# Two-layer hybrid decoder on one core: a first group that starts without the low halves, an output projection by column blocks, and rotary embedding wholly on VectorE

## What is computed

```
h = rms_norm(x, attn_norm); proj = h @ w_in                  # 1024 x 3072
q, k of 16 heads of 64 get the rotary embedding:
    out = concat([x1*cos - x2*sin, x2*cos + x1*sin])
out_a = rms_norm(causal attention of heads 0-7); out_d = rms_norm(dilated attention of heads 8-15)
x = x + concat([out_a, out_d]) @ w_out                       # 1024 x 1024
x = x + square(relu(rms_norm(x, mlp_norm) @ w_up)) @ w_down  # 1024 x 4096 x 1024
```

## Time and profile before

| | |
|---|---|
| runs shown | 598.18, 599.14, 599.41 us, median 599.14 |
| the profiled execution | 599.35 us, span of the instructions 597.6 us |
| PE busy | 584.8 us, 98% of the span |
| DVE busy | 401.6 us, 67% |
| ACT busy | 313.9 us, 53% |
| POOL busy | 62.5 us, 10% |

### The profile page before, as it was taken

One profiled execution on the slowest core, in us unless ns is written; L12 is line 12 of the kernel. 1 busy time (PEld: TensorE's weight loads), 2 busy tenths in 40 slices (PEclk: granted clock), 3 DMA queues, 4 the chain that ended last, 5 costly groups with the idle time before them and its releaser, 6 DMA issues.

```text
span 597.6 us, 9254 instructions
## 1 busy us (share of the span) xinstructions
PE 584.8 (98%) x3326; PEld 491.1 (82%) x3326; DVE 401.6 (67%) x649; ACT 313.9 (53%) x532; POOL 62.5 (10%) x67
## 2 busy tenths in 40 slices
PE   8999999999999999999999999999999999999995
PEld 5879876788888888888888898778888888888884
DVE  3896986588655655755389968767775755755634
ACT  4846767465634534435186646774654435435322
POOL 0070240110000000000005225001100000000001
PEclk8999999999999999999999999999999999999999
DMA  8946343437756466465245634440877465465201
GB/s 306 362 143 212 99 160 95 141 129 252 253 182 238 142 200 220 145 237 180 71 161 192 212 100 183 141 141 13 268 247 247 143 220 199 151 231 179 106 0 70
DMA packets 58844, 104.20 MB, mean 174 GB/s; under 512 B 1808, under 2 KB 35136, under 8 KB 58816
## 3 DMA queue, kind: packets, MB, share of 16 engines
q1 hardware_dynamic: 58320, 103.03, 51.3%
q10 hardware_dynamic: 496, 0.81, 0.5%
HBM read 102.79 MB, written 1.05 MB: 174 GB/s over the span
## 4 chain that ended last, share of the span: by engine, by line
PE 88%; DVE 4%; ACT 4%; issue 2%; DMA 1%; POOL 1%; POOLq 0%; ACTq 0%; DVEq 0%
PE psum L1164 20%; PE psum L952 15%; PE psum L954 14%; PE psum L953 14%; PE psum L1167 10%; PE psum L973 6%; PE psum L978 3%; PE psum L1099 2%; PE psum L1119 1%; PE psum L1137 1%; PE psum L959 1%; ACT w_hi L498 1%; DVE w_lo L670 1%; DMA x<-in_x 1%; PE psum L1140 1%
## 5 line engine op out<-in xcount | busy, mean ns | idle before, releaser
L670 DVE TENSOR_TENSOR w_lo<-raw,w_hi 128x1024 fp32r<-128x1024 f32 x188 | 228.5, 1248 | 50.9 <-ACT w_hi L498 50.9
L498 ACT CAST w_hi<-raw 128x1024 fp32r<-128x1024 f32 x188 | 186.6, 1048 | 0.4 <-PE psum L978 0.3
L1164 PE MATMUL psum<-xt,w_hi 128*128 128x512 f32 x512 | 160.7, 395 | 0.0
L952 PE MATMUL psum<-w_hi,ot_hi 128*128 128x512 f32 x320 | 127.2, 397 | 1.5 <-ACT v L566 1.5
L953 PE MATMUL psum<-w_lo,ot_hi 128*128 128x512 f32 x320 | 124.8, 390 | 0.0
L954 PE MATMUL psum<-w_hi,ot_lo 128*128 128x512 f32 x320 | 124.7, 390 | 0.0
L1167 PEld LDWEIGHTS psum<-xt,w_lo 128*128 128x128 f32 x512 | 96.2, 188 | 22.4
L1167 PE MATMUL psum<-xt,w_lo 128*128 128x256 f32 x512 | 100.6, 278 | 0.0
L1164 PEld LDWEIGHTS psum<-xt,w_hi 128*128 128x128 f32 x512 | 80.2, 189 | 2.4
L614 ACT COPY up_cross<-psum 128x512 f32<-128x512 f32 x32 | 18.8, 587 | 118.7 <-PE psum L1167 118.7
L845 DVE TENSOR_TENSOR up_cross<-psum,up_cross 128x512 f32<-128x512 f32 x32 | 22.1, 691 | 74.1 <-ACT up_cross L614 74.1
(11 more groups left out here) (91 smaller groups left out, 593.8 us busy)
## 6 DMA issues: line engine op xcount, KB each, us to landing
raw<-in_w_up SPq DMA_DIRECT2D x32, 1024.0 KB, 5.6
raw<-in_w_down SPq DMA_DIRECT2D x32, 1024.0 KB, 6.7
raw<-in_w_in SPq DMA_DIRECT2D x21, 1024.0 KB, 5.2
raw<-in_w_out SPq DMA_DIRECT2D x8, 1024.0 KB, 4.8
raw<-in_w_in SPq DMA_DIRECT2D x3, 512.0 KB, 8.1
raw<-in_w_in SPq DMA_DIRECT2D x4, 256.0 KB, 4.8
out<-x SPq DMA_DIRECT2D x3, 256.0 KB, 2.4
x<-in_x SPq DMA_DIRECT2D x2, 256.0 KB, 4.8
```

Source lines behind the costliest of these rows:

```text
L498: act.copy(dst, src).then_inc(hi_done, 1)
L670: dve.tensor_tensor(lo_t, src, hi_t, ALU.subtract).then_inc(split_done, 1)
L952: pe.matmul(out, s_hi, m_hi, start=first, stop=False)
L1164: pe.matmul(up_banks[b][:, f, :], w_hi[:, slot, cols[f]], xt[:, k, :, :].rearrange("p a b -> p (a b)"), start=k == 0, stop=False)
```

## The change

It touches five places. (1) The first six tiles of group 0 in layer 0 are multiplied in the order high x, low weights, low x, with the 512-column matmul in two of 256; four zero matmuls ahead (zero weights) clear the banks; DVE makes each tile's low weights before the low x. (2) `ROPE_ROW` goes from step 10 to 11 and the rotary table entries from 11, 12, 13 to 12, 13, 14. (3) The rotary products become one operation of 1024 elements and their sum one of 512, both on DVE; the table that they read has four rows (cos, cos, sin, minus sin), written by three operations; POOL has no part in it. (4) The output projection of steps 48 to 55 goes t, n, k instead of t, k, n, and frees its four units in the last block. (5) The turning of the last four heads' probabilities and the last product with v come one step later, and squares are always taken one step after the high part.

```diff
-PT_AT = {s + 3: h for s, h in QK_AT.items()}
-PV_AT = {29: (0, 1), 42: (2, 3), 50: (4, 5), 55: (6, 7)}
+PT_AT = {s + 3 + h // 12: h for s, h in QK_AT.items()}
+PV_AT = {29: (0, 1), 42: (2, 3), 50: (4, 5), 56: (6, 7)}
-SQUARES_LATE = {56: (6, 7)}
+SQUARES_LATE = {30: (0, 1), 43: (2, 3), 51: (4, 5), 57: (6, 7)}
-SUM_AT = {8: (0, 0), 9: (0, 1), 12: (1, 0), 16: (1, 1), 36: (4, 0), 40: (4, 1)}
+SUM_AT = {8: (0, 0), 9: (0, 1), 14: (1, 0), 16: (1, 1), 36: (4, 0), 40: (4, 1)}
-ROPE_ROW = 10
-ROPE_AT = {11: (0, 0), 12: (0, 1), 13: (1, 0), 17: (1, 1), 28: (3, 0), 32: (3, 1), 37: (4, 0), 41: (4, 1)}
+ROPE_ROW = 11
+ROPE_AT = {12: (0, 0), 13: (0, 1), 14: (1, 0), 17: (1, 1), 28: (3, 0), 32: (3, 1), 37: (4, 0), 41: (4, 1)}
...
-            def rope_sum(l, g, hg):
-                j = ROPE_GROUPS[g]
-                pool.wait_ge(rope_terms, qk_half(l, g, hg) + 1)
...
-                pool.tensor_tensor(dst[:, 0, :], a[:, 0, :], b[:, 1, :], ALU.subtract)
-                pool.tensor_tensor(dst[:, 1, :], a[:, 1, :], b[:, 0, :], ALU.add).then_inc(rope_done, 1)
...
-                dve.tensor_tensor(rope_r[:, :, :], rope_tab[:, :, :],
-                                  row_bank[:, 0:SEQ].unsqueeze(1).broadcast_to([P, 2, SEQ]), ALU.mult)\
-                    .then_inc(rope_scaled, 1)
+                row = row_bank[:, 0:SEQ].unsqueeze(1)
+                dve.tensor_tensor(rope_r[:, 0:2, :], rope_tab[:, 0:1, :].broadcast_to([P, 2, SEQ]),
+                                  row.broadcast_to([P, 2, SEQ]), ALU.mult)
+                dve.tensor_tensor(rope_r[:, 2:3, :], rope_tab[:, 1:2, :], row, ALU.mult)
+                dve.scalar_tensor_tensor(out=rope_r[:, 3:4, :], in0=rope_tab[:, 1:2, :], scalar=-1.0, in1=row,
+                                         op0=ALU.mult, op1=ALU.mult).then_inc(rope_scaled, 1)
...
-                dve.tensor_tensor(a, raw_qk, cos, ALU.mult)
-                dve.tensor_tensor(b, raw_qk, sin, ALU.mult).then_inc(rope_terms, 1)
+                terms = rope_a[:, :, :].rearrange("p a (i t) -> p a i t", i=2)
+                dve.tensor_tensor(terms, raw_qk.broadcast_to([P, 2, 2, SEQ]),
+                                  rope_r[:, :, :].rearrange("p (a i) t -> p a i t", a=2), ALU.mult).then_inc(rope_terms, 1)
+                if l > 0 or j > 1:
...
+                dve.wait_ge(rope_terms, n + 1)
+                dve.tensor_tensor((q_t, k_t)[j % 2][:, hg, :, :], terms[:, 0, :, :], terms[:, 1, ::-1, :], ALU.add)\
+                    .then_inc(rope_done, 1)
...
                     for k in range(4):
+                        tile_to_lo(k)
                         x_lo(k)
-                        tile_to_lo(k)
...
                 pe.wait_ge((tile_hi, hi_done)[k % 2], k // 2 + 1)
-                pe.wait_ge(turned_lo, k + 1)
+                pe.wait_ge(turned_hi, k + 1)
                 for hg, i in tiles:
-                    with_both(0, k, slot, hg, i)
+                    pe.matmul(qk_banks(0, hg)[:, i, 0:SEQ], feature_tile(w_hi, k, slot, hg, i), xt[:, k, 0, :],
+                              start=False, stop=False)
...
+                pe.wait_ge(turned_lo, k + 1)
+                for hg, i in tiles:
+                    last = pe.matmul(qk_banks(0, hg)[:, i, SEQ:2 * SEQ], feature_tile(w_hi, k, slot, hg, i),
+                                     xt[:, k, 1, :], start=False, stop=False)
...
-                    for k in range(4):
-                        u = 2 * IN_CHUNKS + k
-                        if t == 0:
-                            unit_ready(l, u // 2, k % 2)
-                            pe.wait_ge(o_split, l * PAIRS + k + 1)
-                        for n in range(2):
-                            if k == 0 and t == 0:
-                                pe.wait_ge(v_done, l * 4 + 2 + n + 1)
...
+                    for n in range(2):
+                        if t == 0:
+                            pe.wait_ge(v_done, l * 4 + 2 + n + 1)
+                        else:
+
+                            pe.wait_ge(masked, l * N_HEADS + SET_HEADS + 4 + n + 1)
+                        for k in range(4):
+                            u = 2 * IN_CHUNKS + k
+                            if (t, n) == (0, 0):
+                                unit_ready(l, u // 2, k % 2)
+                                pe.wait_ge(o_split, l * PAIRS + k + 1)
                             mm = project_out(l, acc_d, k, u, t, n, k == 0, k == 3)
-                        if t == TOK - 1:
-                            mm.then_inc(weights_used, 1)
-                        attention(l, 4 * IN_CHUNKS + 4 * t + k)
+                            if (t, n) == (1, 1):
+                                mm.then_inc(weights_used, 1)
+                            if k % 2 == 1:
+                                attention(l, 4 * IN_CHUNKS + 4 * t + 2 * n + k // 2)
```

More of the change, by code:

```diff
@@ L156, in hybrid_kernel @@
         rope_tab = sb("rope_tab", [2, SEQ])
-        rope_r = sb("rope_r", [2, SEQ])
+        rope_r = sb("rope_r", [4, SEQ])
         layer_gains = 2 * KT + 2 * 4
@@ L419, in inverse_rms @@
                                    ALU.pow).then_inc(rstd_done, 1)
-            def rope_sum(l, g, hg):
-                j = ROPE_GROUPS[g]
-                pool.wait_ge(rope_terms, qk_half(l, g, hg) + 1)
-                if l > 0 or j > 1:
-                    pool.wait_ge(scored, l * N_HEADS + (4 * hg + 4 if j > 1 else 4 * hg + 4 - SET_HEADS))
-                dst = (q_t, k_t)[j % 2][:, hg, :, :]
-                a, b = (r[:, hg, :].rearrange("p (i t) -> p i t", i=2) for r in (rope_a, rope_b))
-                pool.tensor_tensor(dst[:, 0, :], a[:, 0, :], b[:, 1, :], ALU.subtract)
-                pool.tensor_tensor(dst[:, 1, :], a[:, 1, :], b[:, 0, :], ALU.add).then_inc(rope_done, 1)
             def add_squares(l, p):
@@ L451, in _ @@
                 inverse_rms(l, ST_X)
-                for g in (0, 1, 3):
-                    for hg in range(2):
-                        rope_sum(l, g, hg)
-                        if (g, hg) == (3, 0):
-                            add_squares(l, 1)
-                for hg in range(2):
-                    rope_sum(l, 4, hg)
-                add_squares(l, 2)
-                add_squares(l, 3)
+                for p in range(1, SET_PAIRS):
+                    add_squares(l, p)
                 inverse_rms(l, ST_D)
@@ L743, in _ @@
             dve.memset(squares[:, 1, 0:BANK], 1.0).then_inc(ones_set, 1)
+            dve.memset(squares[:, 0, BANK:BANK + P], 0.0).then_inc(ones_set, 1)
             dve.wait_ge(gains_turned, 1)
@@ L937, in _ @@
             pe.sem_inc(pv_done, 4)
-            pe.wait_ge(ones_set, 1)
+            pe.wait_ge(ones_set, 2)
             def warm_up(n):
                 for _ in range(n):
-                    pe.matmul(banks[1][:, :], squares[:, 1, 0:P], squares[:, 1, 0:BANK], start=True, stop=True)
-            warm_up(8)
+                    pe.matmul(banks[6][:, :], squares[:, 1, 0:P], squares[:, 1, 0:BANK], start=True, stop=True)
+            warm_up(4)
+            for n in range(4):
+                pe.matmul(banks[n][:, :], squares[:, 0, BANK:BANK + P], squares[:, 1, 0:BANK], start=True, stop=False)
             pe.wait_ge(ident_made, 1)
@@ L969, in feature_tile, with with_both @@
                 return w[:, slot, first:first + P]
-            def with_both(g, k, slot, hg, i):
+            def with_both(g, k, slot, hg, i, first):
                 return pe.matmul(qk_banks(g, hg)[:, i, :], feature_tile(w_hi, k, slot, hg, i),
-                                 xt[:, k, :, :].rearrange("p a b -> p (a b)"), start=k == 0, stop=False)
+                                 xt[:, k, :, :].rearrange("p a b -> p (a b)"), start=first, stop=False)
             def with_lo(g, k, slot, hg, i):
@@ L1007, in first_project_in @@
                 for hg, i in tiles:
-                    last = with_lo(0, k, slot, hg, i)
+                    with_lo(0, k, slot, hg, i)
+                pe.wait_ge(turned_lo, k + 1)
+                for hg, i in tiles:
+                    last = pe.matmul(qk_banks(0, hg)[:, i, SEQ:2 * SEQ], feature_tile(w_hi, k, slot, hg, i),
+                                     xt[:, k, 1, :], start=False, stop=False)
                 if k % 2 == 1:
```

23 lines of the change are left out of this document (10 added, 13 removed).

## The result

The changed kernel takes **600.71 us** (599.12 to 601.40, 21 runs) where the kernel before, on the same chips, takes 598.46 (598.01 to 600.17, 21 runs). The ratio is 1.0024, with an interval of 1.0017 to 1.0032: slower, by 1.0 to 1.9 us, where 1.4 us less was forecast. The runs of both kernels fall into two groups. The changed one has 8 runs of 599.1 to 599.7, at a mean granted clock of 0.997 to 0.998, and 13 of 600.5 to 601.4 at 0.994 to 0.996; the kernel before has 12 from 598.0 to 598.6 and 9 from 599.0 up. The profiled executions are both of the upper group: 599.35 before and 600.96 after, 1.6 apart, with a mean granted clock of 0.995 in both. A mean clock is a rough sign of where the half clock stood: it also counts a stretch of half clock at the very end of the program, where PE has nothing more to do.

The account below looks back on a forecast made before the run. PE, busy 98% of the span, bounds the kernel, so only its waits can be won. Against the profiled 599.35: -1.8 -1.1 +1.1 +0.4 = -1.4, so 597.95, stated as 597.8 us; range 595.8 to 599.6.

Parts of the forecast that it names:

- The projection, -1.8 and -1.1: Steps 48 and 52, both layers: column blocks remove waits for v (0.90 x 2), later turning wins 0.55 x 2.
- the price of the cast in ACT's queue: Projection: ACT's cast for unit 24's place, about 1.05 us, taken as hidden; uncovered it costs 0.4 to 0.9 a layer.
- DVE's prices: Rotary on DVE: product 1.22, sum 0.68, a half 2.0 us where the next operation waits, table 1.5.
- the rival with DVE in time: Step 19: DVE not late if waits between its operations cost nothing; time 596.0, or 595.5 with whole start; chance 0.24.
- the dear product: Rotary product on DVE costs more than a plain 1024-element operation; at 0.54 more a half, 3.2 us in all.
- Step 19 in layer 1, +1.1: PE waits for unit 11's low weights from DVE, starting at 330.1 instead of 329.02: a new wait of 1.1 us.
- Step 19 in layer 0, +0.4: DVE ends unit 11 at 39.0, so PE starts at 39.15 instead of 38.73, 0.4 us later.
- I carry 0.6 us into DVE's stretch: Start, layer 0: PE's 0.6 us earlier start moves DVE's first sum from 25.75 to 25.15; bounds 0 and 1.1.
- come again: Behind the first tile, at 9 to 10 us: PE's half-clock stretch (granted 0.50) was assumed to recur.
- PE only stands longer at step 19: Layer 0: the start's 0.6, the row's 0.3 and the wait for unit 10 are all eaten at step 19.
- Halves behind step 17, "I cost them at nothing": Four halves at steps 17 to 41: DVE's extra 0.8 us each lies beside PE work, priced at nothing.
- The rival "slower": Rotary product on DVE costs 0.54 more a half, three halves a layer ahead of unit 11: 601.0 us; chance 0.12.

Follow-up runs that it names:

- the start alone: Kernel before with part 1 only (high x, low weights, low x order in the first tiles): 599.25 us, ratio 1.0010.
- filling it: The change plus ten unused 512-column matmuls ahead of step 19 in layer 0: 599.44 us, ratio 1.0010 to the kernel before.
- the old order: The change without part 2, rotary row at step 10 and table entries as before: 599.09 us, ratio 1.0008 to the kernel before.
- rotary alone: Kernel before with part 3 only, rotary products and sum on DVE, step tables as before: 600.84 us, ratio 1.0031.
- taking back the squares of step 30: The change with the third rotary half at step 16, behind unit 11, and the first squares at step 29 again: 597.46 us, ratio 0.9973 to before.
- the projection alone: Kernel before with parts 4 and 5 only, column blocks and later turning and squares: 596.43 us, ratio 0.9952.
- The two fastest versions: Kernel before with parts 4 and 5: 596.43 us, ratio 0.9952; kernel before with parts 1, 4 and 5: 596.34 us, ratio 0.9956.
- the best one with the rotary on VectorE: The change with the third rotary half behind unit 11 and the first squares where they were: 597.46 us, ratio 0.9973 to before.

## Why the prediction was wrong

Against the profiled execution the sum said -1.4, and +1.6 was measured; 3.0 us are to be placed.

- **The projection, -1.8 and -1.1: right.** Alone it gives 2.9 by the ledger (1.45 a layer) and 2.6 between the medians, with 1.0 for the column blocks and 0.5 for the turning in layer 0 (0.9 and 0.55 were forecast). In the changed kernel 0.14 is left of the wait for the turning (106.13 to 106.50 less 0.23), where 0.2 was forecast; the price of the cast in ACT's queue did not come.
- **DVE's prices: right.** The product 1.22, the sum 0.69, a half 2.04, the table 1.38 to the start of the product (28.93 to 30.31; 1.5 forecast), with 0.41 and 0.42 at 256 elements. By the formula of the Trainium skill, VectorE: DVE Perf Modes, section "The TRN2 errata", an estimate for 256 elements is 0.42, and the trace agrees. The gap behind a wait is 0.04 (30.31 + 1.22 to 31.57), and not the overlap of 0.08 without one. So the rival with DVE in time, which needed waits that cost nothing, falls, and so does the dear product.
- **Step 19 in layer 1, +1.1: right in place and size.** 1.18, and 1.3 up to the first scores (the first matmul behind a wait takes 0.33 instead of 0.23).
- **Step 19 in layer 0, +0.4: the first step that failed.** "I carry 0.6 us into DVE's stretch": 0.3 arrived (25.46 against 25.75), since the chunk for units 8 and 9 landed no earlier (22.92 in the change, 22.32 before, and the start alone shows the same). And the 0.3 were not part 1's gain: without part 1 and with a start at the full clock DVE came to this point at 24.57 to 24.79. So step 19 is 0.58 late, 0.2 more. The words "PE only stands longer at step 19" were true, and I gave that no price.
- **The half clock behind that wait, not in the sum: 1.55.** This is the largest item. I read the half clock of the start in the earlier trace rows, which was to "come again", and never asked whether a wait of over 2 us could bring the same. By the two groups it did in 13 of 21 runs. That it is the wait is shown by filling it (no half clock, 12 of 12 runs in the lower group, 1.3 less between the medians) and, the other way round, by the old order. The Trainium skill, TensorE: Matmul & The Clock Gate, section "Part 1: The HAM clock gate", ties the clock to how busy PE has been; the trace agrees in that PE was busy for 0.34 of the 2.40 us from 36.8 to 39.2, ahead of the fall at 40.11, and that the filled wait brought no fall.
- **Halves behind step 17, "I cost them at nothing": failed, +0.7.** Two losses of 0.35 at step 35. Of each, the rotary half alone makes 0.12 (rotary alone), and taking back the squares of step 30 removes 0.23: that part is DVE's new length together with POOL's addition, which holds DVE by 0.25. The squares moved without the rotary work on DVE cost nothing (the projection alone). I had priced the interference of the rotary sums that goes, and not that of the squares that part 5 moves.
- **The base.** The profiled execution of before had a half clock in its start and lies 0.9 above the median of 21 runs. The lead that PE gets when this half clock is missing, 1.4 to 1.7 us at the fourth tile (12.39 to 12.66 in the three kernels without part 1 that show it, against 14.04), is waited away at the row, at step 18 or at step 19 in each of them.

The layer-0 and layer-1 misses at step 19 (0.2 each), the half clock (1.55) and step 35 (0.7) are 2.65 of the 3.0; 0.4 more lies outside the span (2.1 against 1.7 us). The rival "slower" had the sign and the time (601.0 against the median, 600.71 measured), but by luck: the product was never dear.

What is worth keeping is the projection. The two fastest versions are 596.43 and 596.34, both with the rotary sums on POOL; the best one with the rotary on VectorE is 597.46. So in every order tried the rotary work on VectorE costs time against the projection alone, 1.0 us at best between the medians. Not settled is why 0.7, 0.6 and 2.3 us of idle time in layer 0 bring the half clock in some executions, and 1.9 and 1.7 in none of 11. That the start alone is 0.1% slower than before fits its later chunk: the slow start, which it takes away, costs DVE about as much as the later chunk does, so it would only take the fast runs of before away, as it did with the projection's two of 595.3. No such run of before was profiled, so this is argued and not shown.

## What to carry to other kernels

A lead that one engine gains upstream is worth only what the next late engine leaves of it; follow it to the first transfer that lands no earlier, or even later. The 2.3 us that TensorE waited here cost up to 1.55 more in clock behind them, so an edit that only "makes it stand longer" needs a price, and where the idle time cannot be removed it may pay to split it or to fill it. When an engine gets more to do, look at the order of its queue first: moving one rotary half behind one unit of weights was worth 2.4 to 2.7 us, about as much as the projection, while the start was worth nothing.
